# Softmax factors by pairs of steps, rotations further ahead, and an output product kept in two halves: a two-block transformer kernel on one core

## What is computed

```python
h = rms_norm(x, norm_mix_pre[l])
proj = h @ w_in[l]
qa, ka, va, qb, kb, vb = jnp.split(proj, SPLITS, axis=-1)
qa = apply_rope(rms_norm(qa.reshape(B, S, N_HEADS_A, HEAD_DIM), q_norm_a[l]), ang_axial)
ka = apply_rope(rms_norm(ka.reshape(B, S, N_KV_A, HEAD_DIM), k_norm_a[l]), ang_axial)
out_a = global_attention(qa, ka, va)
...
out_b = window_attention(qb, kb, vb, sink_b[l])
mixed = jnp.concatenate([rms_norm(out_a, group_norm_a[l]),
                         rms_norm(out_b, group_norm_b[l])], axis=-1) @ w_out[l]
x = x + rms_norm(mixed, norm_mix_post[l])
```

## Time and profile before

| | |
|---|---|
| median of 3 runs | 1240.77 us (1240.4 to 1242.35) |
| profiled execution | 1240.76 us, its span from the first to the last instruction 1238.9 us |
| mean granted PE clock | 0.971 of full speed |
| busy: PE, PE weight load, DVE, ACT, POOL | 92%, 75%, 54%, 40%, 12% of the span |
| chain that ended last | PE 81%, DVE 11%, ACT 4% of the span |

### The profile page before, as it was taken

One profiled execution on the slowest core, in us unless ns is written; L12 is line 12 of the kernel. 1 busy time (PEld: TensorE's weight loads), 2 busy tenths in 40 slices (PEclk: granted clock), 3 DMA queues, 4 the chain that ended last, 5 costly groups with the idle time before them and its releaser, 6 DMA issues.

```text
span 1238.9 us, 14579 instructions
## 1 busy us (share of the span) xinstructions
PE 1145.4 (92%) x5104; PEld 923.3 (75%) x5104; DVE 667.8 (54%) x1022; ACT 495.4 (40%) x811; POOL 154.1 (12%) x166
## 2 busy tenths in 40 slices
PE   6888887879999999999978999789999999999996
PEld 5566766667888888888866887567888888888884
DVE  5787775567544444433348787737444444443332
ACT  5666675435332323322234265734323322332221
POOL 1355555012000000000003001300000000000001
PEclk9899988989999999999999998999999999999998
DMA  6311100321322222222330221003223222223211
GB/s 253 116 51 43 52 26 1 118 86 52 119 97 89 102 102 101 85 102 103 103 107 24 96 102 69 1 1 136 85 102 102 87 99 93 93 102 102 102 51 68
DMA packets 31464, 106.03 MB, mean 86 GB/s; under 512 B 4032, under 2 KB 4672, under 8 KB 31296
## 3 DMA queue, kind: packets, MB, share of 16 engines
q1 hardware_dynamic: 31088, 104.99, 24.6%
q10 hardware_dynamic: 336, 0.52, 0.1%
HBM read 100.78 MB, written 2.10 MB: 83 GB/s over the span
## 4 chain that ended last, share of the span: by engine, by line
PE 81%; DVE 11%; ACT 4%; issue 2%; POOL 1%; DMA 0%; DVEq 0%; SPq 0%; ACTq 0%
PE bank L451 25%; PE bank L452 25%; PE bank L453 25%; PE bank L871 2%; PE bank L861 1%; DVE hl L1411 1%; DVE ta L1403 1%; DVE wl L373 1%; DVE xres L1405 1%; DVE q L1025 1%; PE bank L888 1%; PE bank L887 1%; ACT pr L1340 1%; DVE pr L923 1%; DVE kl L1028 1%
## 5 line engine op out<-in xcount | busy, mean ns | idle before, releaser
L451 PE MATMUL bank<-hh,wh 128*128 128x512 f32 x936 | 373.6, 399 | 27.0 <-DVE hl L1411 25.2
L373 DVE TENSOR_TENSOR wl<-raw,wh 128x1024 fp32r<-128x1024 f32 x181 | 224.5, 1241 | 321.4 <-ACT wh L365 321.1
L365 ACT ACTIVATE wh<-raw 128x1024 fp32r<-128x1024 f32 x181 | 191.4, 1059 | 463.6 <-PE bank L453 322.7
L452 PE MATMUL bank<-hl,wh 128*128 128x512 f32 x936 | 368.5, 394 | 0.0
L453 PE MATMUL bank<-hh,wl 128*128 128x512 f32 x936 | 368.5, 394 | 0.0
L451 PEld LDWEIGHTS bank<-hh,wh 128*128 128x128 f32 x936 | 178.3, 191 | 69.8 <-issue 23.7
L452 PEld LDWEIGHTS bank<-hl,wh 128*128 128x128 f32 x936 | 178.5, 191 | 38.1 <-issue 1.7
L453 PEld LDWEIGHTS bank<-hh,wl 128*128 128x128 f32 x936 | 178.1, 190 | 37.7
L451 PE MATMUL bank<-gh,wh 128*128 128x512 f32 x352 | 139.1, 395 | 0.0
L453 PE MATMUL bank<-gh,wl 128*128 128x512 f32 x352 | 139.1, 395 | 0.0
L452 PE MATMUL bank<-gl,wh 128*128 128x512 f32 x352 | 139.1, 395 | 0.0
(11 more groups left out here) (200 smaller groups left out, 1392.1 us busy)
## 6 DMA issues: line engine op xcount, KB each, us to landing
raw<-weights SPq DMA_DIRECT2D x181, 512.0 KB, 3.2
xres<-x_t SPq DMA_DIRECT2D x8, 512.0 KB, 7.0
sw<-ta SPq DMA_DIRECT2D x36, 64.0 KB, 2.0
out_t<-final SPq DMA_DIRECT2D x8, 256.0 KB, 2.2
rope<-angles SPq DMA_DIRECT2D x1, 1024.0 KB, 10.7
sw<-ta ACTq DMA_DIRECT2D x4, 64.0 KB, 2.2
wp<-pool_weights ACTq DMA_DIRECT2D x1, 256.0 KB, 3.4
mats_raw<-matrices SPq DMA_DIRECT2D x1, 128.0 KB, 8.8
```

The lines of the kernel that those rows point to most:

```text
L365: act.activation(wh[:, j, :, :], raw[:, j, :, :], ACT.Copy).then_inc(high_split, 1)
L373: v.tensor_tensor(wl[:, j, :, :], raw[:, j, :, :], wh[:, j, :, :].bitcast(F32), ALU.subtract)\
L451: pe.matmul(bank[:, :], wh[:, slot, b, :], ah[:, k, :], start=first and n == 0, stop=False)
L452: pe.matmul(bank[:, :], wh[:, slot, b, :], al[:, k, :], start=False, stop=False)
```

## The change

- **Startup.** The two first tiles are rotated and split one to two ticks earlier, ahead of the projection of tile 3 on DVE; weight splits of the first chunks move; four pieces of tile 4 move from tick -2 to ticks 0 and 1.
- **Keys.** DVE makes the low part of a k tile once per half (two instructions, not four), and ACT copies it to the other half (`act_keys_low`, a new semaphore `keys`).
- **Factors by pairs.** `rden` is computed every second tick for two steps, not every fourth for four; POOL multiplies two steps at a time. With sinks, ACT's `esink` and DVE's `rsum` addition are also made by pairs.
- **Rotations.** `free(t)` now avoids odd ticks; `ADD` comes in the tick of `SIN`. `LOW` of tiles 3, 4, 6, 7, 9, 10, 11 moves from 6, 7, 22, 30, 39, 46, 54 to 4, 11, 19, 27, 37, 43, 49, of tile 5 (keys) from 14 to 15. The heads need them at ticks 8, 16, 24, 32, 40, 48, 56 and 24.
- **Output product.** Input tiles are split unscaled (`act_mix_high`, `vec_mix_low`), seven of eight inside the ticks. The halves k < 4 and k >= 4 of an output tile go to banks of their own (`out_banks`). When read, each half is multiplied by its group's factor and the two are added (`vec_take1`); ACT squares the sum (`act_take1`). The four `group_scale` of POOL and four of DVE are gone. In ticks there are 14 pieces (ticks 52 to 72) for the 16 of before.

The diff, cut to its core:

```diff
-    while t >= 5 and t % 4 in (1, 2):
-        t += 1
-    return t
+    return t + 1 if t >= 3 and t % 2 else t
...
-ADD = {m: free(SIN[m] + 1) for m in ROPED}
+ADD = SIN
...
+MIX = {i: WHOLE[i] + 1 for i in range(7)}
+MIX.update({0: 49, 1: 50, 2: 51})
+
+OUT_PIECES = {52: [(0, 0)], 53: [(1, 0)], 54: [(0, 1)], 55: [(1, 1)], 56: [(0, 2)], 57: [(1, 2)], 58: [(0, 3)], 59: [(1, 3)],
+              65: [(0, 4)], 66: [(1, 4)], 67: [(0, 5)], 68: [(1, 5)], 71: [(0, 6)], 72: [(1, 6)]}
...
+        def out_banks(d):
+            return ((banks[0], banks[2]), (banks[1], banks[3]), (banks[4], banks[5]), (banks[6], banks[7]))[d % 4]
+
+        def out_piece(pe, d, k):
+            slot = (CHUNK0["out1"] + d) % RING
+            bank = out_banks(d)[k // 4]
+            pe.wait_ge(mixsplit1.low, MIX_ORDER.index(k) + 1)
+            pe.matmul(bank[:, :], wh[:, slot, k, :], mix_high(k), start=k % 4 == 0, stop=False)
+            pe.matmul(bank[:, :], wh[:, slot, k, :], mix_low(k), start=False, stop=False)
+            return pe.matmul(bank[:, :], wl[:, slot, k, :], mix_high(k), start=False, stop=k % 4 == 3)
...
         def pe_out1(pe):
...
+            for k in range(4):
+                out_piece(pe, 2, k)
+            for k in range(4, 7):
+                out_piece(pe, 2, k)
             pe.wait_ge(n_gb.added, 3)
-            pe.matmul(bank[:, :], ones[:, :], sq[:, :], start=True, stop=False)
+            pe.wait_ge(at1.added, len(HEADS1))
+            pe.matmul(banks[6][:, :], ones[:, :], sq[:, :], start=True, stop=False)
             pe.wait_ge(n_gb.squared, 1)
-            pe.matmul(bank[:, :], ones[:, :], rh[:, :], start=False, stop=True).then_inc(n_gb.summed, 1)
...
+            pe.matmul(banks[6][:, :], ones[:, :], rh[:, :], start=False, stop=True).then_inc(n_gb.summed, 1)
+            for d in range(3):
+                out_piece(pe, d, 7).then_inc(used, 1)
+            for d in range(3, 8):
+                slot_wait(pe, c0 + d)
+                if d == 3:
+                    pe.wait_ge(n_gb.ready, 1)
+                else:
+                    pe.wait_ge(bank_read, len(IN1) + d - 3)
+                for k in range(8):
+                    ins = out_piece(pe, d, k)
                 ins.then_inc(used, 1)
...
-            if t % 4 == 1 and 5 <= t <= STEPS + 1:
-                s = t // 4 - 1
-                c = slice(4 * s % 8, 4 * s % 8 + 4)
-                v.wait_ge(at1.exped, 4 * s + 4)
+            if t % 2 and 3 <= t <= STEPS + 1:
+
+                n = t - 3
+                s = n // 4
+                c = slice(n % 8, n % 8 + 2)
+                v.wait_ge(at1.exped, n + 2)
...
+        def act_keys_low(act, m):
+            i = IN1[m][2]
+            act.wait_ge(f1.part.low, parted(m))
+            for par, own, other in pair():
+                ins = act.activation(kl1[i][other, par, :], kl1[i][own, par, :].bitcast(F32), ACT.Copy)
+            ins.then_inc(f1.keys, 1)
...
+        def act_tail1(act):
             act.wait_ge(at1.added, len(HEADS1))
             act.wait_ge(n_gb.added, 3)
             act.activation(rh[:, :], xres[:, 7, :], ACT.Square).then_inc(n_gb.squared, 1)
...
+            act_mix_high(act, 7)
+            act_rstd(act, n_gb, banks[6], sq, 512)
...
+        def vec_take1(v):
+            c0 = CHUNK0["out1"]
+            for d in range(KT):
+                vec_split(v, c0 + d + RING)
+                full, window = out_banks(d)
+                v.wait_ge(used, c0 + d + 1)
+                if d == 0:
+                    v.wait_ge(n_ga.ready, 1)
+                    v.wait_ge(n_gb.ready, 1)
+                v.tensor_tensor(ta[:, d % 2, :], full[:, :], rstd[:, :], ALU.mult).then_inc(mixed_parts, 1)
+                v.tensor_tensor(tb[:, d % 2, :], window[:, :], sq[:, :], ALU.mult).then_inc(bank_read, 1)
+                if d >= 1:
+                    add_square(v, n_mp, d - 1, acc)
+                v.wait_ge(mixed_parts, d + 1)
+                v.wait_ge(bank_read, len(IN1) + d + 1)
+                v.tensor_tensor(mixed1[:, d, :], ta[:, d % 2, :], tb[:, d % 2, :], ALU.add).then_inc(mixed_there, 1)
+
+        def act_take1(act):
+            for d in range(KT):
+                act_split(act, CHUNK0["out1"] + d + RING)
+                act.wait_ge(mixed_there, d + 1)
+                act_square(act, n_mp, d, mixed1[:, d, :])
```

193 lines of the change are left out of this document (90 added, 103 removed).

## The result

The changed kernel takes **1234.86 us** (median of 8 runs, 1230.2 to 1237.2) against 1240.8 us before (8 runs on the same chip): ratio 0.9947, 95% interval 0.9931 to 0.9964. It is 5.9 us faster; 14.5 us were forecast. The runs scatter by 7 us, those of before in this comparison by 3 us. They were run on several chips, on which the kernel before had medians of 1239.3 to 1240.8 us, so a difference of 1 us between medians tells little. The profiled execution took 1236.36 us with a span of 1234.6 us (before 1238.9).

The account below looks back on a forecast made before the run. The prediction took waits and the lower clock level, not work, to bound the second half of the ticks. Last tick 21 us earlier, end 6.5 us later: 1240.8 - 21 + 6.5 = 1226.3 us, its own range 1221 to 1232.

Parts of the forecast that it names:

- Startup: Ahead of tick 0: earlier rotations and fewer low-part instructions bring first scores at 44, not 51.2: -7.2 us.
- Ticks 0 to 7: First stage: clock gives back 1.5 us, short query waits shrink, two more pieces cost 1.4: sum -1.0 us.
- Ticks 8 to 39: Second stage: 4.2 us query wait, 3 of maxima waits and 1.5 of clock go, pieces add 3.5: -5.2 us.
- Ticks 40 to 55: Third stage: waits and clock would give 26.8 us, but DVE's added work bounds it at 32.3: -2.3 us.
- I take half of that as new, 6: Ticks: of 13 us of short waits left, half return as new waits, so the last tick ends 21 us earlier.
- The second rival: Ticks give half, 10 us, as DVE sets the pace and maxima waits replace query waits: 1237.3 us, chance 0.20.
- Ticks 56 to 75: Last stage: 3.2 us of mixed-tile waits, 4 of clock and 4.2 of pieces go: -11.4 us.
- Behind the last tick: After the ticks: ACT and DVE by turns take 5.35 us a tile, so the norm's factor comes 6.5 us later.
- the first rival: Behind the last tick the round is no bound, factor at 44.5 us behind the last tick: 1217.7 us, chance 0.10.
- Pairs: Ticks: factors by pairs can pay only by making room for rotations; by themselves they bring nothing.
- Rival 3: Ticks: DVE, slowed behind POOL by 0.6 us an instruction, becomes the bound; ticks give 3 or less: 1245 us, chance 0.12.

Follow-up runs that it names:

- e15: The changed kernel measured once more with nothing edited: 1232.4 us.
- e11: Changed kernel with only the weight splits behind tiles 10 and 11 one tick later: 1229.8 us.
- e4: Changed kernel with the parts of mixed tiles 0 to 4 at ticks 53 to 58 and the output product's eight pieces at 56 to 61: 1233.8 us.
- e7: Changed kernel with the old tables of tiles 5 to 11 and mixed parts later as in e4: 1230.5 us.
- e8: Changed kernel with weight splits behind tiles 10 and 11 and v's middle product a tick later, plus the edit of e2: 1220.5 us.
- e12: e7 (changed kernel with old tables of tiles 5 to 11) plus the edit of e2: 1219.4 us.
- e1: Changed kernel, behind the last tick ACT splits the next weight chunk before waiting for the current tile's sum: 1226.6 us.
- e2: Changed kernel, behind the last tick DVE's low part of a weight chunk stands behind the sum of the two halves: 1224.1 us.
- e5: Kernel before with only the reciprocals, sink additions and POOL's multiplications by pairs: 1236.2 us.
- e10: Changed kernel with POOL multiplying only the first 8 columns of each pr, so the output differs: 1227.4 us.
- e9: e8 with the factors by fours in place of pairs: 1215.7 us.

## Why the prediction was half right

- **Startup**, -7.2 forecast, -5.8 measured: the mechanism was right. Within the same code tick 0 moves from 44.9 to 47.2, so the miss of 1.4 is within that scatter. In e15's trace the first scores come at 43.35, 7.8 us earlier than before; PE's granted clock around them is 1.00 there and 0.51 in the trace above, where the two products for tile 3's squares take 2.02 us for 1.10.
- **Ticks 0 to 7**, -1.0 forecast, +1.1: PE is busy 0.9 us more, with eight products more by the records for six, and the clock rose only from 0.88 to 0.93 where 1.5 of the 1.9 us were credited. Its standing time did not fall.
- **Ticks 8 to 39**, -5.2 forecast, -1.1: the 4.2 us query wait went, and the 3 us taken from the waits for maxima came as forecast in this stage (4.5 to 1.3). But PE stands for 8.7 us in place of 12.9, 4.2 less where the sum has 7.2: 2.1 us more for v and 1.5 for the turned tiles' low parts stand in their place. PE's busy time rose by 3.1, for 2.0 in the sum (3.5 of pieces less 1.5 of clock).
- **Ticks 40 to 55**, -2.3 forecast, +2.9: the largest miss. DVE's busy time was forecast within 1 us and the clock rose to 0.91 as said (0.86 in e15's trace, which has the same length of stage). What failed is "So DVE is what bounds here: I take 32.3". In this order the engine was not filled to the 97% that I took: it stood for 5.1 us (most of its idle time in the ticks ends with ACT's `pth`, 20.1 us from 46 to 190), and PE for 9.7 us, some 6 of them for maxima. e11 shows one place, 1.8 to 2.3 us of this stage for one tick's shift of two splits. e4 shows that the five mixed parts which I had priced are not it: they and their pieces only change the stage in which they are paid.
- **"I take half of that as new, 6"**: this is the step that made the forecast wrong. Of the 27.1 us, 13.9 did not come. PE's new waits in the ticks are 10.1 us. The sum had room for 4.0 of them: these 6, less the 3 taken off the waits for maxima, and 1.0 more in ticks 40 to 55, where DVE's bound added 5.5 us and 4.5 of clock had been taken off. PE's busy time, without those 4.5 us of clock, came nearly as forecast (5.2 less for 5.6). e7 tells what the term should have held: the new tables of tiles 5 to 11, on which most of the 7.5 us for ticks 8 to 55 rest, cost 3 net beside pairs. That is part of the 7.9 us missing beyond the 6, and the new tables with the splits and v a tick later recover as much (e8 against e12); why pairs and new tables hinder each other stays open. The second rival had the size (ticks give 10; they gave 13.2) and the form (waits for maxima in place of those for queries), but not its reason: DVE's busy share in ticks 8 to 39 fell to 63.5 of 84.5 us.
- **Ticks 56 to 75**, -11.4 forecast, -10.3: right. PE stands for 2.2 us less (3.2 forecast) and is busy for 8.1 less (8.2), at a clock of 1.00 for 0.85. This stage and the startup are all of the gain ahead of the last tick's end. No run has the unscaled mixed parts alone, so their share is argued, and 4.2 us of it are pieces that only moved to other stages.
- **Behind the last tick**, +6.5 forecast, +7.0: right, and e1 and e2 show the mechanism. Round 5.28 us (5.35), PE idle 11.6 us (12), last square 49.0 us behind the last tick (49.9). The step from that square to the factor was mis-sized, 4.6 us for 3.2: I put PE's sums down "as before", and behind the stand they ran at a granted clock of 0.50. That the end is off by only 0.5 us is partly luck, as the 0.9 too much for the round cancels most of it. The same 1.4 us are most of the difference of e1 (46.2) to the first rival (44.5).
- **Pairs**: "the factors by pairs can pay only by making room for the rotations" failed. On the kernel before they gained 3.5 us alone (e5), and beside the new tables, for which they were to make room, they cost.
- **The remainder**: the forecast was 14.5, the profiled spans differ by 4.3. Of these 10.2 us, 7.8 are the last tick's end (21 for 13.2), 0.5 the end, and 1.9 the rest of the program, in which nothing was changed; the second trace of the same code has 0.0 there.
- **Rival 3**, POOL holding DVE, came nowhere near its size: e10 puts the price of 19.4 us of POOL's multiplications at 4 us, and against the kernel before the query parts became shorter and only the weight splits longer, by 0.18 us. The section "SBUF: two separate sides" of "SBUF — State Buffer" in the Trainium skill has the loser wait for the whole instruction of the other; of DVE's it names those in a 2-port performance mode and those with two SBUF inputs. e10 agrees in which instructions change (`q` and `wl`, not `ptl`) and in sign, but in the mean it was 0.17 and 0.07 us (POOL's rotations stayed), where the third rival took 0.6.

Taking the two misses of sign together: had the tables been left, and the splits of the end put in the right order, the change would have given 20 us (e12). Leaving the factors by fours instead, and keeping the new tables with the splits a tick later, gave 23.5 (e9, 1215.7 for 1239.3).

## What to carry to other kernels

Moving a late instruction earlier on in-order engines is worth only what its new neighbours let through: list what each tick holds on each engine and look for two long instructions ahead of one that frees a bank, before crediting the wait that goes. A product that finishes earlier is worth nothing if two engines read it by turns; put each engine's work for the next round where it waits for this one (e2: one line moved, 9.6 us). Test each part of a change alone, and then in pairs of parts: factors by pairs were worth about -3.5 us on the old tables and +3 to +5 on the new ones, and the new tables +3 or nothing beside pairs and -4 beside fours. A test of one part tells its worth only beside the others as they are. And when the borders of a stage can be drawn at two engines, look at both cuts before saying in which stage time was lost (e4).

## What was not expected of the hardware

An unchanged stretch scatters: from the factor on the rest of the program took 967.8 to 972.2 us in these 18 traces, and two traces of the same code differ by 2.3 us at the maximum of tick 0 and 1.9 in the rest, but 0.1 in the ticks between. PE's sum of two products was 2.08 us at clock 0.50 behind a stand of 11.57 us, and 1.13 at 1.00 behind one of 1.98, though the sum that followed it took 1.88 at 0.66; the granted clock from 208.8 to 262.4 is 0.88, and 0.86 in the 38 us behind it. POOL's multiplication of 8 columns took 0.47 us in the mean, of up to 512 columns 0.83, so most of a small one is fixed cost.
